# Identity products on TensorE around the last turn and the routing, and expert weights loaded in halves

## What is computed

```python
x = layer_norm(DN_ALPHA * x + gate1 * mixed, p['ln1_g'], p['ln1_b'])
h = layer_norm(x) * (1.0 + scale2) + shift2
lg = h @ p['w_rg'] + p['b_rg']              # 4 groups
le = h @ p['w_re'] + p['b_re']              # 32 experts; the two best of the best group are taken
hid = silu(h @ w_e1[e]) * (h @ w_e3[e])     # 1024 -> 256, for the tokens that chose expert e
y   = (hid * gate) @ w_e2[e]                # 256 -> 1024
x = layer_norm(DN_ALPHA * x + gate2 * y, p['ln2_g'], p['ln2_b'])
```

## Time and profile before

| | us |
|---|---|
| median of 3 runs | 1417.75 |
| lowest, highest | 1416.76, 1420.36 |
| the profiled execution | 1417.07 |
| its span | 1415.3 |
| TensorE (PE) busy in the span | 1259.9 (89%) |
| VectorE (DVE) busy | 561.1 (40%) |
| mean rate of the DMA engines | 155 GB/s |

### The profile page before, as it was taken

How to read it: one execution, slowest core, us unless ns; L and a number is a source line. 1 busy time by engine, 2 the same in 40 slices (tenths; PEclk the granted TensorE clock), 3 DMA queues, 4 the chain that set the end, 5 groups by cost and what they waited for, 6 DMA issues and landing times. The chain is left out here.

```text
span 1415.3 us, 14701 instructions
## 1 busy us (share of the span) xinstructions
PE 1259.9 (89%) x5617; PEld 732.1 (52%) x5617; DVE 561.1 (40%) x1279; ACT 292.1 (21%) x595; POOL 72.0 (5%) x124
## 2 busy tenths in 40 slices
PE   3899999787989899989999999999997499599755
PEld 1455555454566777656666655555445244244212
DVE  5230576678312333433655532011485521011117
ACT  2201454254033233411111210000001011011112
POOL 0000000000000000000000000000300122122100
PEclk9999999988999899999999999999997599899887
DMA  9533234230201202011211113820617499999944
GB/s 374 213 124 134 70 119 162 106 92 21 97 21 51 80 22 54 27 69 53 67 45 45 45 46 112 238 67 23 263 45 287 176 389 421 419 420 417 412 171 201
DMA packets 63214, 219.32 MB, mean 155 GB/s; under 512 B 21209, under 2 KB 32065, under 8 KB 46497
## 3 DMA queue, kind: packets, MB, share of 16 engines
q1 hardware_dynamic: 57808, 206.75, 39.0%
q0 software_dynamic: 5184, 10.50, 2.0%
q10 hardware_dynamic: 144, 1.05, 0.2%
HBM read 208.89 MB, written 17.76 MB: 160 GB/s over the span
## 5 line engine op out<-in xcount | busy, mean ns | idle before, releaser
L501 PE MATMUL bank<-hT,ring 128*128 128x512 f32 x320 | 165.3, 598 | 0.0
L2678 PE MATMUL bank<-ew,xgT 128*64 128x512 f32 (+2 forms) x544 | 132.6, 629 | 27.1 <-issue 25.1
L1667 PE MATMUL bank<-hT,w_ab 128*128 128x512 f32 x256 | 131.1, 594 | 0.4 <-issue 0.4
L2678 PEld LDWEIGHTS bank<-ew,xgT 128*64 128x64 f32 (+2 forms) x544 | 47.7, 146 | 109.2 <-issue 108.4
L955 PE MATMUL bank<-hT,ring 128*128 128x512 f32 x192 | 100.8, 607 | 2.2 <-DVE yA L1449 2.2
L502 PEld LDWEIGHTS bank<-hT,ring 128*128 128x128 f32 x320 | 60.8, 190 | 76.5 <-issue 76.5
L1668 PEld LDWEIGHTS bank<-hT,w_ab 128*128 128x128 f32 x256 | 48.6, 190 | 61.2 <-issue 61.2
L2102 PE MATMUL bank<-w_out,mT 128*128 128x512 f32 x160 | 70.9, 604 | 2.2 <-PEq L1599 2.2
L2693 PE MATMUL bank<-ew,hidT 128*64 128x512 f32 (+2 forms) x272 | 66.9, 621 | 3.8 <-DMA ew<-in_experts 3.0
L2824 DVE SCALAR_TENSOR_TENSOR uh<-uh,bank 128x256 f32<-128x256 f32 x18 | 7.6, 421 | 153.0 <-ACT uh L2763 153.0
L1778 PE MATMUL bank<-hT,w_c 128*128 128x512 f32 x128 | 65.5, 594 | 0.0
(11 more groups left out here) (458 smaller groups left out, 1980.8 us busy)
## 6 DMA issues: line engine op xcount, KB each, us to landing
ew<-in_experts SPq DMA_DIRECT2D x96, 1024.0 KB, 23.9
ring<-in_blocks SPq DMA_DIRECT2D x10, 2048.0 KB, 8.7
mhalf<-in_mods SPq DMA_DIRECT2D x16, 1024.0 KB, 5.0
w_ab<-in_merge SPq DMA_DIRECT2D x16, 768.0 KB, 4.4
mstage<-in_mods SPq DMA_DIRECT2D x3, 2048.0 KB, 18.4
w_c<-in_merge SPq DMA_DIRECT2D x8, 768.0 KB, 4.4
yt<-expert_rows SPq DMA_DIRECT2D x5, 1024.0 KB, 12.3
w_out<-in_w_out SPq DMA_DIRECT2D x1, 4096.0 KB, 12.0
```

The source lines that it names most:

```text
L501: pe.matmul(lat[:, :], w, hT[:, k, P:T], start=(k == 0), stop=(k == KD - 1))
L1667: pe.matmul(bank[5][:, :], w[:, k, :], hT[:, k, P:T], start=(k == 0), stop=(k == KD - 1))
L2678: mm = pe.matmul(bank[2 + n % 2][hs, :], xgT[:, n % 2, k, hs], ew1[w][k // 4][:, 512 * (k % 4):512 * (k % 4) + 512], start=(k == 0), stop= ...
```

## The change

Two things are put in. `filler(pe, n)` issues n products of the 128 x 128 identity with itself into PSUM bank 7, which nobody reads: 10 before and 3 behind the last turn in "out", 22 at the start of "route", 48 behind the rank product and 24 behind the table product. And the two halves of a first-layer load get a semaphore each. TensorE's mark "f1a" says that k 0 to 3 of a unit's first layer are done; the first half of the next load of the slot waits for it alone, the second half for "f1". `ffn1` waits for the first halves before k 0 and for the second ones before k 4. The first two ordered experts are loaded as first half, first half, second half, second half. The expert's number is read before the wait. Numbers, order and size of all other transfers stay.

```diff
-    got_w13 = [nc.alloc_semaphore(f"got_w13_{x}") for x in range(6)]
+    got_w1 = [[nc.alloc_semaphore(f"got_w1_{i}_{x}") for x in range(6)] for i in range(2)]
+    def load_half(sp, e, s, i):
+        sp.dma_start(ew1[s][i][:], e[:, W13 // 2 * i:W13 // 2 * (i + 1)]).then_inc(got_w1[i][s], 16)
...
+    def filler(pe, n):
+
+        for _ in range(n):
+            pe.matmul(bank[7][:, 0:P], ident, ident, start=True, stop=True)
...
+                if i == NT + 1:
+                    filler(pe, 10)
                 if i >= 3:
                     logits(i - 3)
                 if 0 <= i - 2 < NT:
                     turn(i - 2)
+                if i == NT + 1:
+                    filler(pe, 3)
...
+            filler(pe, 22)
             pe.wait_ge(v9.sem, v9.after("mall"))
...
             mm.then_inc(p9.step("rank"), 1)
+            filler(pe, 48)
             pe.wait_ge(v9.sem, v9.after("rhs2"))
...
             mm.then_inc(p9.step("tab"), 1)
+            filler(pe, 24)
...
-    pt_m = Marks("te", ("xT", "hT", "f1", "f2"))
+    pt_m = Marks("te", ("xT", "hT", "f1a", "f1", "f2"))
...
+        def first_half(expert, x, i):
+            sp.wait_ge(pt_m.sem[("f1a", "f1")[i]], user_of(x - 6) + 1)
+            load_half(sp, EXPERT(expert), x % 6, i)
+
+        def first_halves(expert, x):
+            for i in range(2):
+                first_half(expert, x, i)
...
+        def second(expert, x):
+            sp.wait_ge(pt_m.sem["f2"], user_of(x - 6) + 1)
+            load_second(sp, EXPERT(expert), x % 6)
...
+        for i in range(2):
+            for x in (NSTAT, NSTAT + 1):
+                first_half(expert_of(x), x, i)
         for n in range(U_SORT, NP):
-            sorted_loads(load_first, "f1", n)
+            sorted_loads(first_halves, n)
             if n > U_SORT:
-                sorted_loads(load_second, "f2", n - 1)
+                sorted_loads(second, n - 1)
...
         def ffn1(n, halves=4):
-            for h in range(min(halves, len(loads_of(n)))):
-                first_ready(n, h)
...
             for k in range(KD):
+                if k % 4 == 0:
+                    for h in range(min(halves, len(loads_of(n)))):
+                        ready(got_w1[k // 4], 16, n, h)
+                if k == 4:
+                    mm.then_inc(pt_m.sem["f1a"], 1)
                 for hs, w in parts(n):
```

More of the change, by code:

```diff
@@ L2056, in program @@
         (ring_off - 2048, mT1_off, mT1_off + 40960, hT_off, hT_off + 12288, low_off))]
-    got_w13 = [nc.alloc_semaphore(f"got_w13_{x}") for x in range(6)]
+    got_w1 = [[nc.alloc_semaphore(f"got_w1_{i}_{x}") for x in range(6)] for i in range(2)]
     got_w2 = [nc.alloc_semaphore(f"got_w2_{x}") for x in range(6)]
+    def load_half(sp, e, s, i):
+        sp.dma_start(ew1[s][i][:], e[:, W13 // 2 * i:W13 // 2 * (i + 1)]).then_inc(got_w1[i][s], 16)
     def load_first(sp, e, s):
         for i in range(2):
-            sp.dma_start(ew1[s][i][:], e[:, W13 // 2 * i:W13 // 2 * (i + 1)]).then_inc(got_w13[s], 16)
+            load_half(sp, e, s, i)
     def load_second(sp, e, s):
         sp.dma_start(ew2[s][:], e[:, W13:]).then_inc(got_w2[s], 16)
+    def filler(pe, n):
+        for _ in range(n):
+            pe.matmul(bank[7][:, 0:P], ident, ident, start=True, stop=True)
     turns8 = lambda n, *parts: [(x, i - lag) for i in range(n) for lag, names in parts for x in names if 0 <= i - lag < NT]
@@ L2550, in sync_units, with expert_of, sorted_loads, extra_loads @@
     def sync_units(sp):
-        def sorted_loads(load, mark, n):
-            for x in new_loads(n):
[L2553 to L2558, removed]
+        def first_half(expert, x, i):
[4 more added lines that the diff above has]
+                first_half(expert, x, i)
+        def expert_of(x):
+            r = RANKS[x - NSTAT]
+            return sp.value_load(order[0:1, r:r + 1], min_val=0, max_val=NE - 1)
+        def second(expert, x):
+            sp.wait_ge(pt_m.sem["f2"], user_of(x - 6) + 1)
+            load_second(sp, EXPERT(expert), x % 6)
+        def sorted_loads(load, n):
+            for x in new_loads(n):
+                if x > NSTAT + 1 or load is second:
+                    load(expert_of(x), x)
+        def extra_loads(load, n):
             u = 2 * (n - NP)
@@ L2561, in extra_loads @@
                 with sp.If(units > u + h):
-                    sp.wait_ge(pt_m.sem[mark], user_of(x - 6) + 1)
-                    expert = sp.value_load(extra[0:1, 1 + u + h:2 + u + h], min_val=0, max_val=NE - 1)
-                    load(sp, EXPERT(expert), x % 6)
+                    load(sp.value_load(extra[0:1, 1 + u + h:2 + u + h], min_val=0, max_val=NE - 1), x)
+        for i in range(2):
+            for x in (NSTAT, NSTAT + 1):
+                first_half(expert_of(x), x, i)
         for n in range(U_SORT, NP):
-            sorted_loads(load_first, "f1", n)
+            sorted_loads(first_halves, n)
             if n > U_SORT:
-                sorted_loads(load_second, "f2", n - 1)
+                sorted_loads(second, n - 1)
         units = sp.value_load(extra[0:1, 0:1], min_val=0, max_val=NXH)
-        extra_loads(load_first, "f1", NP)
-        sorted_loads(load_second, "f2", NP - 1)
+        extra_loads(first_halves, NP)
+        sorted_loads(second, NP - 1)
         def rest(n):
@@ L2576, in rest @@
                 if n + 1 < NU:
-                    extra_loads(load_first, "f1", n + 1)
-                extra_loads(load_second, "f2", n)
+                    extra_loads(first_halves, n + 1)
+                extra_loads(second, n)
                 if n + 1 < NU:
@@ L2659, in first_ready @@
         def first_ready(n, h):
-            ready(got_w13, 32, n, h)
+            for i in range(2):
+                ready(got_w1[i], 16, n, h)
         def second_ready(n, h):
```

## The result

| | before | after |
|---|---|---|
| median, us | 1417.75 | 1409.59 |
| lowest, highest, us | 1416.68, 1420.36 | 1406.17, 1411.40 |
| profiled execution, its span, us | 1417.07, 1415.3 | 1410.11, 1408.3 |
| mean granted clock of TensorE | 0.944 | 0.957 |

The ratio of after to before is 0.9938, with a 95% interval of 0.9923 to 0.9954: 8 us faster, where 10.7 were forecast. The changed kernel's own times lie 5 us apart.

What follows compares the result with a forecast made beforehand. The prediction took the experts' stage as bound by the weight stream and its late start; terms of 3.4 + 1.1 + 1.1 + 0.9 + 6.3 = 12.8 us, less 2.4 for one clock fall, gave 1407.0 us, range 1403.5 to 1413.0.

Steps and rivals of the forecast that it cites:

- What bounds: Experts' stage: the stream of expert weights sets it, so everything ahead of the first ordered load at 1132.81 us counts.
- (a) to (e): Gains with clock up: end of "out" 3.4 us, ranks 1.1, table 1.1, gathered rows' turn 0.9, halved loads 6.3.
- Does the clock hold: Behind the 48 products, ahead of the table's product: one clock fall costing 2.4 us, leaving 10.4; chance 0.40.
- rival 2: The clock falls at the last turn and again before the table: gain 8.2 us, 1408.9 us; chance 0.17.
- repaired by the 22: A clock fall around the last turn costs 2.2 us, and the 22 products at the route's start repair it.
- rival 5: Identity products stay at 1.2 GHz in front of rank and table products: 1432.6 us; chance 0.06 with lesser forms.
- the first of the signs: Route block: the forecast is wrong if a rank or table product starts late behind identity products.
- The other two: Signs of error: DMA share under 0.9 in the stream's first 20 us; the 14.8 us wait grows by what was won.
- rival 3: The stream runs dry behind TensorE, as slots come free too late: gain 6.3 us, 1410.8 us; chance 0.10.
- The end "is untouched": After the last wait for weights: two units' second layers, the scatter and the final block stay as before.
- Rivals 4 and 5: 4: the clock rises but the last load lands when it did, 1413 to 1419 us, chance 0.08; 5: see rival 5.

Runs made afterwards that it cites:

- after_again: The changed kernel measured once more, unaltered, beside the kernel with the products alone on one chip: median 1407.69 us, ratio to before 0.9923.
- behind_ranks_96: The changed kernel with 96 instead of 48 identity products behind the rank product: 1416.38 us, ratio to before 0.9961.
- release_late: The changed kernel, but the first half of a load waits for the whole first layer: 1410.25 us, 1409.60 without one slow execution, ratio 0.9923.
- products_only: The kernel before with the 107 identity products alone, loads and waits as before: 1408.54 us, ratio 0.9920.
- last_wait_filled: The changed kernel with 24 identity products ahead of the second layer of the last unit but one: 1404.67 us, ratio to before 0.9906.
- quarter_ranks_54: The changed kernel with the first two ordered experts' first-layer weights in quarters and 54 instead of 48 products behind the rank product: 1404.22 us, ratio 0.9900.
- turn_filled: The changed kernel with 2 more identity products ahead of the turn of tile 4 and 4 instead of 3 behind it: 1410.44 us, ratio 0.9934.

## Why the prediction was right, and where it was not

**What bounds.** Right. S to L, the ordered stream of 78 MB, takes 225.7 to 226.4 us in all nine profiles of the table, whether unit 0's product ended 9 us sooner behind M than before (after_again) or 3 us later (behind_ranks_96), with whole loads or halves. Only quarters made it longer.

**(a) to (e) with the clock up.** after_again is that case: M to B 18.06 - 14.60 = 3.5 us (forecast 3.4); the route 20.93 - 19.75 = 1.2 (1.1); table to turn 10.15 - 8.92 = 1.2 (1.1); turn to unit 0's product 2.86 - 1.92 = 0.9 (0.9); issue 10.27 - 3.86 = 6.4 (6.3). The sum is 13.2 where 12.8 stood.

**Does the clock hold.** I took one fall, at the table, for 2.4 us. The profile after has one fall, but at the last turn, rival 2's place. Its price was mis-sized at 2.2 us, "repaired by the 22", for which the prediction gives no working. It is 2.5 in M to B (17.12 - 14.60) and 1.4 more in the route (21.12 - 19.75), as the 22 products, begun at the low clock, take 7.2 us in a gap of 5.4 and the rank product stands behind them. By S it is 3.7 us (52.8 - 49.1). That is rival 5's mechanism in small, and it is the first of the signs by which the prediction said it would be wrong, "if a rank or table product starts late behind identity products": the sign came, and the time stayed in the range. The other two did not: the DMA share is 0.90 in the first 10 us of the stream and 1.01 in the next, and TensorE's wait of 14.8 us did not grow, as its longest there is 9.4 us. The fall at the table costs 11.50 - 8.92 = 2.6 us (2.4). With both, as in rival 2, it is 55.5 - 49.1 = 6.4 instead of 4.6.

The Trainium skill ("TensorE: Matmul & The Clock Gate", Part 1) says that the point of the rise differs between runs of one kernel; by that rule single runs would differ by a few us. The traces agree in the size, with 49.1, 52.8 and 55.5 us from M to S, but what differs in them is where the clock fell. The times of the changed kernel spread over 5.2, 1.5 and 9.4 us in its three series.

**The stream runs dry** (rival 3). Not for halves: S to L is 0.1 us longer, where up to 1 was allowed. With quarters it is 1.2 and 2.3 us longer, but the rows show busy DMA engines at a lower rate in the first stretch, not an empty queue.

**The end "is untouched".** In length nearly so: L to E is 57.0, 56.1 and 55.3 us in the three profiles of the changed kernel and 56.2 before. As a mechanism it is wrong, since 54.2 and 55.0 with the products alone show that it could be shorter and the halves keep it from that. The halves let the last unit of four experts begin when its first halves have landed, so TensorE is ready for the second layer of the last unit but one 2 to 3 us sooner behind S (220.0 to 221.3 us, where it was 223.2 before). It then stands 5.1 us (after) or 6.3 us (after_again) for the last second-layer weights, where it stood 3.0 before and 2.0 and 1.0 with the products alone, and that second layer takes 6.18 and 5.44 us, where it took 5.25 before and 3.64 with the products alone. Why the wait is shorter with the products alone than before is open. release_late has the same wait (5.8 us), so it comes from the two semaphores of arrival and not from the early release. The wait and the layer in after_again, and then in products_only:

```profile
1348.59 5.44 PE L2727 MATMUL bank<-ew,hidT 128*32 128x512 f32 x32 [6.30 <-DMA ew<-in_experts]
```

```profile
1352.27 3.64 PE L2705 MATMUL bank<-ew,hidT 128*32 128x512 f32 x32 [1.98 <-DMA ew<-in_experts]
```

last_wait_filled shows that this is on the path. So of the 4.3 us by which the halves start the stream sooner (8.14 - 3.86 at the same clock), 0.5 us go in S to L and about 2 in the tail; some 2 us are left by the cuts. The medians of one chip have 3.8 us, those of different series nothing.

**Rivals 4 and 5.** What the slowest DMA engine does follows the start, so 4 is out. 5 in full did not occur; behind_ranks_96 shows what products ahead of the table's cost at the high clock, and also that the cover of the 48 products is 1.7 us wide.

So the forecast is right in its mechanism, and two of its terms were wrong: the place and price of the fall, 3.7 us at the last turn instead of 2.4 at the table, and the tail. The profiled execution has 1410.11 where 1406.7 was forecast, 3.4 us more: 1.6 are M, ahead of everything that was changed, 1.3 the fall, 0.9 what is lost behind S, less 0.4 by which the parts (a) to (e) gave more. The median was 2.6 us above the forecast in the first series, but the forecast's own ratio, 0.9924, is inside the interval of each of the three series: how close a median comes to it is in part luck of the series. quarter_ranks_54 and last_wait_filled have the lowest ratios of all, 0.9900 and 0.9906, but their intervals reach to that of the changed kernel. For last_wait_filled the cuts agree with a gain (M to the end 330.3 us, 331.5 in after_again); for quarter_ranks_54 they do not (333.3).

## What to carry to other kernels

Where a stage is set by a stream of loads that never runs dry, look for what holds its first transfer: each us ahead of it was a us where the last wait for weights ended, in both directions, and cutting the first wait in two was worth 3.4 us at the stream's start. Products put in to hold TensorE's clock have to fit into their gap at the low clock too, or to start where the clock is up: 22 of them behind a fall made the next product 1.7 us late. And a gain at one end of a stage lengthens waits at the other; look there for the next fall.

## What the runs showed that was not expected

The wait for the first sums of the final block leaves TensorE at the low clock in every profile without products there (VectorE starts 5.2 to 6.7 us behind them). With 34 identity products around it the sums began at the high clock (1.00 from 1373.2 to 1375.0), yet SyncE's issues of the read back took 1.96 instead of 0.91 us for two, and what was won was lost again. And the start of the whole part, M, wanders from 1068.5 us (quarter_ranks_54) to 1074.7 (turn_filled) between executions of programs that are the same up to there: 6 us, most of what the change is worth. A single span therefore says little about a change of this size. Of the kernel before there is one profile (1070.5 us), so whether M is later on average with the change is not known.
